# A depthwise convolution's taps added two at a time on GpSimd, and a bias load moved into its first tile

## What is computed

```python
for i in range(DEPTH):                       # DEPTH = 2
    proj = rmsnorm(x, norm_mix[i]) @ w_in[i]
    q, k, v, cglu, sc_b, sc_c, sc_h, gates = split(proj)
    y_a = window_attention(q, k, v, sinks[i], bias) @ w_attn_out[i]   # bias: by relative distance
    ca, cb = split(cglu)
    c = ca * sigmoid(cb)
    c = causal_dwconv(c, conv_dw[i]) + conv_dw_bias[i]               # 31 taps per channel
    y_b = silu(layernorm(c)) @ w_conv_out[i]
    y_c = (sc_b * causal_dwconv(sc_c * sc_h, sc_conv[i])) @ w_sc_out[i]   # 3 taps
    x = x + (g0 * y_a + g1 * y_b + g2 * y_c) @ w_mix_out[i]
    x = x + (silu(h2 @ w_gate) * (h2 @ w_up)) @ w_down               # h2 = rmsnorm(x)
    x = x + (p[i] @ w_ple[i]) * sigmoid(rmsnorm(x) @ w_ple_gate[i])
return rmsnorm(x, norm_final)
```

## Time and profile before

| | |
|---|---|
| median of 3 runs | 1177.83 us (1177.38 to 1177.88) |
| profiled execution | 1177.76 us, span of its instructions 1176.0 us |
| busy in the span | PE 97%, DVE 70%, ACT 60%, POOL 36% |
| mean granted TensorE clock | 0.991 of full speed |
| weight loads | 183 of 1 MB in the loop, median 4.8 us to landing |

### The profile page before, as it was taken

One profiled execution on the slowest core, in us unless ns is written; L12 is line 12 of the kernel. 1 busy time (PEld: TensorE's weight loads), 2 busy tenths in 40 slices (PEclk: granted clock), 3 DMA queues, 4 the chain that ended last, 5 costly groups with the idle time before them and its releaser, 6 DMA issues.

```text
span 1176.0 us, 24193 instructions
## 1 busy us (share of the span) xinstructions
PE 1136.9 (97%) x9340; PEld 1121.9 (95%) x9340; DVE 821.8 (70%) x1217; ACT 704.3 (60%) x1139; POOL 425.2 (36%) x405
## 2 busy tenths in 40 slices
PE   6998999998999999999999999999999999999996
PEld 5998999997999999999989999999999999999996
DVE  6786887775766665456699887878776675545657
ACT  5477887764745543444667788876574455434454
POOL 0288668795002000002127886679620200000012
PEclk9998999998999999999999999999999999999998
DMA  8554434444454456455335553435545535645541
GB/s 308 211 194 164 144 109 146 172 166 154 171 195 169 161 196 228 152 179 202 139 126 193 203 180 108 144 123 200 179 173 195 199 125 213 212 153 190 198 144 37
DMA packets 29358, 201.54 MB, mean 171 GB/s; under 512 B 3521, under 2 KB 3713, under 8 KB 5841
## 3 DMA queue, kind: packets, MB, share of 16 engines
q1 hardware_dynamic: 27648, 195.38, 46.9%
q0 software_dynamic: 1088, 4.74, 1.2%
q10 hardware_dynamic: 528, 0.15, 0.1%
HBM read 199.19 MB, written 3.69 MB: 173 GB/s over the span
## 4 chain that ended last, share of the span: by engine, by line
PE 69%; POOL 11%; ACT 8%; DVE 5%; DMA 3%; issue 3%; POOLq 0%; ACTq 0%; DVEq 0%; SPq 0%
PE bank L324 21%; PE bank L326 21%; PE bank L325 21%; POOL pacc L1314 10%; ACT w_hi L553 3%; DMA w_raw<-in_wstream 3%; DVE w_lo L890 2%; ACT cprod L553 1%; POOL sqsum L1325 1%; PE bank L436 1%; PE bank L361 1%; PE bank L362 1%; ACT cv L742 1%; PE bank L364 1%; POOL cv L1314 1%
## 5 line engine op out<-in xcount | busy, mean ns | idle before, releaser
L324 PE MATMUL bank<-h_hi,w_hi 128*128 128x256 f32 x1856 | 533.1, 287 | 3.1 <-DVE w_lo L890 1.7
L325 PE MATMUL bank<-h_lo,w_hi 128*128 128x256 f32 x1856 | 526.7, 284 | 0.0
L326 PE MATMUL bank<-h_hi,w_lo 128*128 128x256 f32 x1856 | 526.6, 284 | 0.0
L890 DVE TENSOR_TENSOR w_lo<-w_raw,w_hi 128x2048 fp32r<-128x2048 f32 x183 | 429.0, 2346 | 111.3 <-ACT w_hi L553 110.9
L553 ACT ACTIVATE w_hi<-w_raw 128x2048 fp32r<-128x2048 f32 (+1 forms) x185 | 351.1, 1900 | 164.0 <-DMA w_raw<-in_wstream 127.1
L324 PEld LDWEIGHTS bank<-h_hi,w_hi 128*128 128x128 f32 x1856 | 357.6, 193 | 10.6 <-issue 6.8
L325 PEld LDWEIGHTS bank<-h_lo,w_hi 128*128 128x128 f32 x1856 | 357.8, 193 | 0.2
L326 PEld LDWEIGHTS bank<-h_hi,w_lo 128*128 128x128 f32 x1856 | 357.6, 193 | 0.0
L1314 POOL TENSOR_TENSOR pacc<-pacc,cprod 128x256 f32<-128x256 f32 x280 | 308.4, 1102 | 82.8 <-ACT cprod L553 45.0
L324 PE MATMUL bank<-act_hi,w_hi 128*128 128x256 f32 x1024 | 292.3, 285 | 4.5 <-DVE w_lo L937 2.9
L325 PE MATMUL bank<-act_lo,w_hi 128*128 128x256 f32 x1024 | 290.8, 284 | 0.0
(11 more groups left out here) (139 smaller groups left out, 860.9 us busy)
## 6 DMA issues: line engine op xcount, KB each, us to landing
w_raw<-in_wstream SPq DMA_DIRECT2D x183, 1024.0 KB, 4.8
rel_bias_rows<-rel_bias_by_distance POOLq DMA_DIRECT2D x1, 2560.0 KB, 17.6
bias<-rel_bias_rows POOLq DMA_DIRECT2D x1, 1536.0 KB, 10.6
xs<-in_x SPq DMA_DIRECT2D x2, 512.0 KB, 4.4
w_raw<-in_wstream SPq DMA_DIRECT2D x2, 512.0 KB, 7.8
out_y<-xs SPq DMA_DIRECT2D x4, 256.0 KB, 2.6
zacc<-in_p POOLq DMA_DIRECT2D x2, 256.0 KB, 4.4
prms<-in_prm SPq DMA_DIRECT2D x1, 328.0 KB, 10.5
```

The lines of the kernel that those rows point to most:

```text
L324: nc.tensor.matmul(o, wh, hi, start=first, stop=False, skip_group_check=True)
L325: nc.tensor.matmul(o, wh, lo, start=False, stop=False, skip_group_check=True)
L326: return nc.tensor.matmul(o, wl, hi, start=False, stop=last, skip_group_check=True)
L890: nc.vector.tensor_tensor(w_lo[:, n % RING, :], w_raw[:, n % RAW_RING, :], f32(w_hi[:, n % RING, :]), ALU.subtract).then_inc(lo_ready, 1)
```

## The change

ACT's products go by pairs: two products side by side are one entry of a ring of two pairs, the same memory as before. `pacc` becomes a pair of accumulators. POOL adds a whole pair to it at once, 512 columns per instruction: 14 such adds, then the two accumulators are added to each other, then the 31st product is added into `cv`. A tile takes 16 POOL instructions where it took 30. ACT waits for the ring once per pair. The products' schedule in layer 0 becomes that of layer 1. POOL goes straight to the first tile; the load of the bias is issued in the midst of it, behind the add of pair 7, and the masks are set behind its last add.

```diff
--- before.py
+++ after.py
@@ -84,10 +84,11 @@
 POOL_CONV = (0, 3, 4, 5, 6)
 EARLY_CONV = (1, 2)
 LATE_CONV = (7,)
-POOL_ADDS = CONV_WIDTH - 1
+PAIRS = (CONV_WIDTH + 1) // 2
+POOL_ADDS = PAIRS
 POOL_STEPS = len(POOL_CONV) * POOL_ADDS
 PRODUCTS = len(POOL_CONV) * CONV_WIDTH
-PROD_RING = 4
+PAIR_RING = 2
 CGLU_TAPS, QKV_TAPS, ATTN_TAPS = 5, 5, 4
 CGLU_PRODUCTS, QKV_PRODUCTS, SC_PRODUCTS = 4, 4, 6
 
@@ -148,8 +149,8 @@
         ple_gates = [gated[:, 0, :], gated[:, 1, :], prod[:, 0, :], prod[:, 1, :]]
 
         cv = sb("cv", [P, DT, CPAD + SEQ])
-        pacc = sb("pacc", [P, SEQ])
-        cprod = sb("cprod", [P, PROD_RING, SEQ])
+        pacc = sb("pacc", [P, 2, SEQ])
+        cprod = sb("cprod", [P, PAIR_RING, 2, SEQ])
         cacc = {1: psum[5][:, 0:SEQ], 2: psum[5][:, SEQ:2 * SEQ], 7: psum[5][:, 0:SEQ]}
         mu = sb("mu", [P, SEQ])
         sq_last = [mu[:, :], sq[:, 1, :]]
@@ -178,7 +179,7 @@
         sinks = sb("sinks", [P, DEPTH, QT * 2 * TB])
         tab = sb("tab", [N_BUCKETS, N_HEADS])
 
-        hot = cprod[0:N_BUCKETS, 0:2, :].rearrange("p a b -> p (a b)")[:, 0:REL]
+        hot = cprod[0:N_BUCKETS, 0, :, :].rearrange("p a b -> p (a b)")[:, 0:REL]
         rel_bias = zacc[0:N_HEADS, :, :].rearrange("p a b -> p (a b)")[:, 0:REL]
         idt = sb("idt", [P, P])
         eps = sb("eps", [P, 1])
@@ -630,10 +631,10 @@
 
                 made = [0]
 
-                def added(n):
-
-                    b, k = divmod(n, CONV_WIDTH)
-                    return L * POOL_STEPS + b * POOL_ADDS + max(k, 1)
+                def pair_added(q):
+
+                    b, i = divmod(q, PAIRS)
+                    return L * POOL_STEPS + b * POOL_ADDS + (i if 0 < i < PAIRS - 1 else 1 if i == 0 else PAIRS)
 
                 def conv_products(upto):
 
@@ -642,10 +643,11 @@
                         t = POOL_CONV[b]
                         if k == 0:
                             wait_read(act, L, 2 * t + 1, (2 * t + 1) % BANKS)
-                        if n >= PROD_RING:
-                            act.wait_ge(pool_step, added(n - PROD_RING))
+                        q = b * PAIRS + k // 2
+                        if q >= PAIR_RING and k % 2 == 0:
+                            act.wait_ge(pool_step, pair_added(q - PAIR_RING))
                         w = CONV_W + t * CONV_WIDTH + k
-                        copy(cprod[:, n % PROD_RING, :], cv[:, t, k:k + SEQ], scale=prms[:, L, w:w + 1],
+                        copy(cprod[:, q % PAIR_RING, k % 2, :], cv[:, t, k:k + SEQ], scale=prms[:, L, w:w + 1],
                              **(dict(bias=prms[:, L, CONV_B + t:CONV_B + t + 1]) if k == 0 else {})).then_inc(prod_ready, 1)
                         made[0] = n + 1
 
@@ -665,9 +667,9 @@
                         raw_activate(t, 2 * t, ACT.Sigmoid)
                     if t > 0:
                         after_chunk(t - 1)
-                        conv_products(CGLU_PRODUCTS * (t if L else max(1, t - 3)))
-                before_qkv, qkv_products = (CGLU_PRODUCTS * (DT - 1), QKV_PRODUCTS) if L else (CGLU_PRODUCTS * (DT - 4), QKV_PRODUCTS + 1)
-                before_sc = before_qkv + qkv_products * (KT + QT // 2)
+                        conv_products(CGLU_PRODUCTS * t)
+                before_qkv = CGLU_PRODUCTS * (DT - 1)
+                before_sc = before_qkv + QKV_PRODUCTS * (KT + QT // 2)
                 for s in range(2 * KT + QT):
                     g = S0["qkv"] + s
                     wait_strip(act, L, g)
@@ -676,7 +678,7 @@
                          ).then_inc(bank_read[g % BANKS], 1)
                     if s % 2:
                         after_chunk(C0["qkv"] + s // 2 - 1)
-                        conv_products(before_qkv + qkv_products * (s // 2 + 1))
+                        conv_products(before_qkv + QKV_PRODUCTS * (s // 2 + 1))
                 act.wait_ge(vt_done, L + 1)
                 copy(v_tok[:, :, :], psum[6][:, 0:TB * KT * P].rearrange("p (b f) -> p b f", b=TB)).then_inc(vtok_ready, 1)
 
@@ -1289,29 +1291,46 @@
 
             pool.dma_start(rel_rows, bass.AP(tensor=rel_dram.tensor, offset=0, ap=[[REL, N_HEADS], [0, P], [1, REL]])
                            ).then_inc(rel_stored, 16)
-            pool.wait_ge(rel_stored, 32)
-
             skewed = bass.AP(tensor=rel_rows.tensor, offset=P - 1, ap=[[REL - 1, P], [P * REL, N_HEADS], [1, KEYS]])
-            pool.dma_start(bias[:, :, :], skewed).then_inc(bias_in, 16)
-            pool.wait_ge(bias_in, 16)
-
-            nc.gpsimd.memset(bias[0:CHUNK, :, P:KEYS], NEG_INF).then_inc(bias_ready, 1)
-            pool.wait_ge(bias_ready, 1)
-            nc.gpsimd.memset(bias[CHUNK:P, :, 0:CHUNK], NEG_INF).then_inc(bias_ready, 1)
-            pool.wait_ge(bias_ready, 2)
+
+            def load_bias():
+
+                pool.wait_ge(rel_stored, 32)
+                pool.dma_start(bias[:, :, :], skewed).then_inc(bias_in, 16)
+
+            def mask_bias():
+
+                pool.wait_ge(bias_in, 16)
+                nc.gpsimd.memset(bias[0:CHUNK, :, P:KEYS], NEG_INF).then_inc(bias_ready, 1)
+                pool.wait_ge(bias_ready, 1)
+                nc.gpsimd.memset(bias[CHUNK:P, :, 0:CHUNK], NEG_INF).then_inc(bias_ready, 1)
+                pool.wait_ge(bias_ready, 2)
+
             pool.wait_ge(dve_set, 1)
 
             for L in range(DEPTH):
 
                 for b, t in enumerate(POOL_CONV):
-                    for k in range(1, CONV_WIDTH):
-                        n = b * CONV_WIDTH + k
-                        pool.wait_ge(prod_ready, L * PRODUCTS + n + 1)
-                        if n > 1:
-                            pool.wait_ge(pool_step, L * POOL_STEPS + b * POOL_ADDS + k - 1)
-                        a = cprod[:, (n - 1) % PROD_RING, :] if k == 1 else pacc[:, :]
-                        o = pacc[:, :] if k < POOL_ADDS else cv[:, t, CPAD:]
-                        nc.gpsimd.tensor_tensor(o, a, cprod[:, n % PROD_RING, :], ALU.add).then_inc(pool_step, 1)
+                    made, done = L * PRODUCTS + b * CONV_WIDTH, L * POOL_STEPS + b * POOL_ADDS
+
+                    def pair(i):
+                        return cprod[:, (b * PAIRS + i) % PAIR_RING, :, :]
+
+                    for i in range(1, PAIRS - 1):
+                        if L == b == 0 and i == PAIRS // 2:
+                            load_bias()
+                        pool.wait_ge(prod_ready, made + 2 * i + 2)
+                        if i > 1:
+                            pool.wait_ge(pool_step, done + i - 1)
+                        nc.gpsimd.tensor_tensor(pacc[:, :, :], pair(0) if i == 1 else pacc[:, :, :], pair(i),
+                                                ALU.add).then_inc(pool_step, 1)
+                    pool.wait_ge(pool_step, done + PAIRS - 2)
+                    nc.gpsimd.tensor_tensor(pacc[:, 0, :], pacc[:, 0, :], pacc[:, 1, :], ALU.add).then_inc(pool_step, 1)
+                    pool.wait_ge(prod_ready, made + CONV_WIDTH)
+                    pool.wait_ge(pool_step, done + PAIRS - 1)
+                    nc.gpsimd.tensor_tensor(cv[:, t, CPAD:], pacc[:, 0, :], pair(PAIRS - 1)[:, 0, :], ALU.add).then_inc(pool_step, 1)
+                    if L == b == 0:
+                        mask_bias()
                 pool.wait_ge(pool_step, (L + 1) * POOL_STEPS)
 
                 for n, t in enumerate(POOL_CONV[1:] + EARLY_CONV + LATE_CONV):
```

## The result

The changed kernel takes 1185.85 us (median of 4 runs, 1184.2 to 1188.05) where the kernel before takes 1177.61 in the same comparison (1177.16 to 1177.88): 1.007 of it, with a 95% interval of 1.0054 to 1.0086. It is slower by 8 us; 1162.0 was forecast, faster by 16.

The account below looks back on a forecast made before the run. PE was taken as the bound, POOL mattering only where PE waits for it. 1177.76 us less 15.25 (layer 0's waits and clock) and 1.1 (weight load), plus 0.6 (locks), gave 1162.0 us; range 1159 to 1169.5.

Parts of the forecast that it names:

- Part 6: ACT's wait on a ring of two pairs, once per pair: POOL needs 4.9 us per 5.68 us step, so no cost.
- Part 5: The lock: wide POOL adds hold DVE's two-SBUF-input operations, at most 1.9 us more per attention chunk; 0.6 us added over all.
- Part 4: Wide POOL adds take 1.37 us each, saving 3.6 us per tile, 18 per layer; this buys margin, no time.
- The margin at line 491: POOL's last channel sum was to end over 10 us before PE needs it, in both layers, up from 1.3 us.
- Parts 1 and 3: Bias load and masks moved into tile 0 cost the path nothing; the weight load's 1.15 us wait at 48 us goes, -1.1 us.
- Part 2: Layer 1's product schedule in layer 0 removes the waits at lines 421 and 491 and their lower clock: 15.25 us.
- B: Rival: early conv taps still late at line 421 in layer 0, from ACT's wait or held DVE; 1168.9 us at most; chance 0.12.
- D: Rival: slower by locks, POOL's wide adds and DVE alternating, strips waiting for banks; 1186 us, chance 0.06 (half of that, 1170, 0.04).

Follow-up runs that it names:

- narrow_sched: The kernel before, still with narrow adds and a ring of four products, plus the moved bias load and masks and layer 1's schedule in layer 0: 1163.8 us.
- narrow_pairwait: narrow_sched with ACT waiting for the ring once per pair, so its four products are freed by pairs; adds stay narrow: 1173.2 us.
- pairs_whole: The changed kernel, still two pairs, with each call of conv_products ending on a whole pair: 1171.5 us.
- pairs_products_first: The changed kernel, still two pairs, with ACT making its products ahead of the chunk's w_hi in the cglu and QKV steps: 1180.1 us.
- narrow_ring6: narrow_sched with six narrow products in the ring instead of four, the last two in sq: 1161.9 us, again 1161.6 us.

## Why the prediction was wrong

- **Part 6 failed, and with it the forecast.** It said that two pairs cost POOL 4.9 us per step of 5.68, "so the ring is free when ACT comes back. Nothing." The rate was right: POOL is idle 1.93 us in each step. But I compared rates and never placed the call's end in the ring. In the QKV stretch, with 31 taps behind them, all calls of four end in the midst of a pair, and in the attention stretch every other call of three, so ACT asks for a slot whose add needs a product of the same call, and that add stands behind `w_lo`. The cost is 2.32 us per step and a step of 6.36 us. The rows to see it were there: rows 6 had the hold beside `w_lo`, and the kernel's code the 31 taps and the calls of four. Of the pairs' 22 us, 9.4 come from freeing by pairs alone, shown with narrow adds, and 12.6 from the longer add, which lengthens that wait; 2.5 to 2.9 of them are there with a long ring too. A third pair takes 21.5 away.
- **Part 5 was right in kind and too small.** I added 0.6 us over all for DVE held by wide adds; with ring enough for both it is 2.5 to 2.9 us. The longest `w_lo` takes 3.39 us, within the 3.5 that I gave. The other direction, `w_lo` holding the add that ACT waits for, stood in part 6 as 1.9 us of POOL's time and as nothing of ACT's.
- **Part 4: the add.** The wide add takes 1.30 us at the median where I took 1.37 from the rows; the estimate of 1.30 that stands beside it came out. The Trainium skill (GPSIMD Engine Reference, section 3.1) has 2.6 cycles per element, and 256 columns more cost 1.301 - 0.742 = 0.56 us, 2.6 cycles of 1.2 GHz each, so the trace agrees. That rate alone makes 1.11 us for 512; the other 0.19 is no figure of that page, it is what the narrow add of 0.742 takes beyond the rate. The group of these adds:

```profile
L1325 POOL TENSOR_TENSOR pacc<-pacc,cprod x130: 1267/1301/3407, 43.1 to 833.0; 128x512 f32<-128x512 f32 x130
```

- **The margin at line 491** was to be over 10 us in both layers; it is 4.5 in each, since ACT's products, not POOL, now set the pace: in the last tiles POOL is idle 0.5 to 0.7 us before its adds, waiting for ACT. These rows of POOL's timeline have the load, the first mask and the last sums; 260.98 + 6.65 = 267.63 and 838.76 + 6.64 = 845.40 stand against PE's 272.17 and 849.95:

```profile
56.95 1.19 POOL L1299 DMA_DIRECT2D bias<-rel_bias_rows  x1
...
81.57 0.94 POOL L1304 MEMSET bias<- 64x1024 f32 x1
...
260.98 6.65 POOL L1344 TENSOR_TENSOR sqsum<-sqsum,cv 128x256 f32<-128x256 f32 x6
...
838.76 6.64 POOL L1344 TENSOR_TENSOR sqsum<-sqsum,cv 128x256 f32<-128x256 f32 x6
```

- **Parts 1 and 3 held as a sum, but not "cost on the path: nothing".** The load goes out at 56.95 us, 2 to 7 us later than I put it, and the masks at 81.57 for 75. PE waits for neither directly, and the wait at 48 us is gone. But the weight load that now collides takes 9.17 us, and in the changed kernel the chain that ended last runs from it over ACT's `w_hi` of 69.71, POOL's adds and the two masks into the QKV steps. So both have a share in layer 0's late taps, 4.86 us where layer 1, with no bias load, has 1.40. In narrow_sched, with the same load and masks, the wait at line 421 is 0.86 and 0 us, so the share is small where ACT has room to catch up. The load in the chain:

```profile
60.51 9.17 DMA w_raw<-in_wstream
```

- **Part 2 held where the ring allows it.** Without pairs, the wait at line 491 goes, that at line 421 falls to 0.86 us, and layer 0 takes layer 1's time from scores to mean within 2.2 us. narrow_sched's 1163.8 us stands beside the 1161.4 us that the sum gives without the 0.6 for locks.
- **The rivals.** B named the place, taps late at line 421 because ACT waits for POOL, with a chance of 0.12, but priced it as no more than layer 0's old wait. It came in both layers, 4.86 and 1.40 us, and the larger loss came behind it, in the attention stretch. D, slower by the lock, had 0.06, and its 1186 us is the measured time, but by luck: it stands for strips that wait because DVE is held by wide adds, which is worth 2.9 us.

Where the loss lies can be read from the profiled executions (us):

| | narrow_sched | narrow_pairwait | pairs_whole | pairs_products_first | changed kernel |
|---|---|---|---|---|---|
| first scores, layer 0, start | 100.33 | 102.56 | 100.77 | 103.46 | 104.22 |
| first scores to mean, layer 0 | 160.68 | 161.72 | 162.89 | 165.28 | 167.95 |
| first scores to mean, layer 1 | 158.52 | 161.95 | 162.85 | 164.20 | 167.33 |
| span | 1162.2 | 1169.2 | 1169.2 | 1178.3 | 1183.8 |

Of the 21.6 us between narrow_sched and the changed kernel 16.1 lie between first scores and mean; of the 14.6 between narrow_pairwait and the changed kernel 11.6 do. So the step of 6.36 us, which is the part that was taken to pieces, accounts directly for the smaller share. What stays open is how much of the attention stretch's loss is made there and how much comes from ACT entering it late. Both seem to have a part: pairs_products_first leaves the stretch's own order as it is and shortens it by 2.7 and 3.1 us, while pairs_whole, late by 0.4 us only, is still 2.2 and 4.3 us longer there than narrow_sched. The lower clock behind the wait of 4.86 us, a mean of 0.53 in the 6 us after it, is in layer 0's length too. No run changes the one without the other, so neither size was measured.

## What to carry to other kernels

When a ring's entries are made larger, don't compare rates: walk one call of the producer through the ring, at each phase that the counts allow (here 31 taps against calls of four), and ask which add must be done and whether that add needs what the same call has just made. A hand-over that groups two items frees them one item later. One more group of slots took 21.5 us off, in memory that was free, and calls that end on a group 14.3 us without any. Half as many instructions on an engine that isn't the bound bought nothing, and each longer one held a neighbour longer.

## What the runs showed of the hardware

- A two-input add on POOL takes 0.742 us at 256 columns and 1.30 at 512, so, taken as a fixed part and one per column, about 0.18 us of it doesn't grow with the size; a memset of one element takes 0.11.
- DVE's one-input `TENSOR_SCALAR` from SBUF to SBUF, too, is held by POOL's wide adds: 0.38 us beside narrow ones, 0.80 in the mean beside wide ones. I had looked for this in operations with two inputs only.
- After PE's wait of 4.86 us the granted clock of the 100 to 120 slice is 0.83, as after the 4.25 us of before. In narrow_sched's trace the wait there is 0.86 us, and the clock stays at 1.00 behind it; it falls, to 0.57 from 118 to 120 us, only after a later wait of 1.39 us for the softmax (line 447, `v_tok` by `probs_t`), which ends at 115.83 us. In narrow_ring6's trace a wait of 1.41 us at the same instruction ends at 115.09 us, and the clock stays at 1.00 to 128 us. So the length of a single wait doesn't say whether the clock falls.
